# Linear attention with staged weights: bias copies issued later, the next head's weights loaded a piece per chunk, the scores' transpose placed further back

## The reference, cut to what matters

```python
u = h @ w_in                                  # q, k, v, r and a low-rank gate a1
glog = log_sigmoid(a1 @ w_a2 + b_a) / GLA_TAU
bc = cumsum(glog)                             # in a chunk
o_inter = (q * exp(bc)) @ S
att[t, s] = sum_d q[t, d] * k[s, d] * exp(bc[t, d] - bc[s, d])     # s <= t
o = o_inter + att @ v
S = exp(b_last) * S + (k * exp(b_last - bc)).T @ v
out = (rmsnorm(o) * norm_g * silu(r)) @ w_out
```

## Time and profile before

| | |
|---|---|
| median of three runs | 2278.31 us (2277.18 to 2278.43) |
| the profiled execution's own time | 2276.93 us |
| its span, first to last instruction | 2275.2 us |
| TensorE matmuls busy | 2171.4 us (95%), 12858 instructions |
| TensorE's mean granted clock | 0.983 of full speed |
| VectorE, ScalarE, GpSimd busy | 1386.6, 1137.7, 1046.7 us |
| linear attention in the span | from 756 to about 1433 us |

### The profile page before, as it was taken

One profiled execution on the slowest core, in us unless ns is written; L12 is line 12 of the kernel. 1 busy time (PEld: TensorE's weight loads), 2 busy tenths in 40 slices (PEclk: granted clock), 3 DMA queues, 4 the chain that ended last, 5 costly groups with the idle time before them and its releaser, 6 DMA issues. The chain is left out here.

```text
span 2275.2 us, 34224 instructions
## 1 busy us (share of the span) xinstructions
PE 2171.4 (95%) x12858; PEld 1089.0 (48%) x12858; DVE 1386.6 (61%) x2174; ACT 1137.7 (50%) x2165; POOL 1046.7 (46%) x790
## 2 busy tenths in 40 slices
PE   8999999999899869999999999899899997999998
PEld 4555555553444434454444444344455553444443
DVE  6999999987564424534544444567558884345322
ACT  7766666676773424433444534333358885334111
POOL 2988888887888121212112121276248886000000
PEclk9999999999999889999999999899999999999999
DMA  5011011033344320121301113365536664103222
GB/s 217 29 47 47 27 45 43 27 117 119 103 137 169 77 56 18 53 52 17 88 16 28 22 30 69 107 161 144 153 72 121 120 103 78 45 10 102 84 101 93
DMA packets 237723, 178.99 MB, mean 79 GB/s; under 512 B 188847, under 2 KB 208943, under 8 KB 236536
## 3 DMA queue, kind: packets, MB, share of 16 engines
q1 hardware_dynamic: 237560, 176.81, 28.9%
HBM read 96.65 MB, written 35.80 MB: 58 GB/s over the span
## 5 line engine op out<-in xcount | busy, mean ns | idle before, releaser
L1179 DVE SCALAR_TENSOR_TENSOR cv_tap_sum<-cv_glu,cv_prm,cv_tap_sum 128x1024 f32<-128x1024 f32 x326 | 418.9, 1288 | 11.9 <-ACT cv_tap_sum L667 2.4
L932 POOL TENSOR_TENSOR mixed<-mixed,cv_tap_products 128x1024 f32<-128x1024 f32 x153 | 364.0, 2379 | 77.7 <-ACT cv_tap_products L682 62.2
L101 PE MATMUL cv_proj<-H_hi,cv_w_ga 128*128 128x416 f16 (+1 forms) x640 | 217.0, 339 | 8.1 <-DVE H_lo L1152 8.1
L102 PE MATMUL cv_proj<-H_lo,cv_w_ga 128*128 128x416 f16 (+1 forms) x640 | 217.0, 339 | 0.0
L103 PE MATMUL cv_proj<-H_hi,cv_w_ga 128*128 128x416 f16 (+1 forms) x640 | 217.0, 339 | 0.0
L101 PE MATMUL gm_vr<-gm_wvr_hi,H_hi 128*128 128x512 f16 x512 | 194.7, 380 | 0.0
L102 PE MATMUL gm_vr<-gm_wvr_lo,H_hi 128*128 128x512 f16 x512 | 194.0, 379 | 0.0
L103 PE MATMUL gm_vr<-gm_wvr_hi,H_lo 128*128 128x512 f16 x512 | 194.0, 379 | 0.0
L1978 POOL TENSOR_TENSOR gm_q_inter<-gm_q_rel,gm_block_decays 128x512 f32<-128x512 f32 x16 | 16.8, 1047 | 350.1 <-ACT gm_block_decays L2068 350.1
L2084 ACT ACTIVATE gm_v_r<-gm_vr 128x256 f16<-128x256 f32 x68 | 26.0, 383 | 291.8 <-PE gm_vr L103 271.4
L682 ACT ACTIVATE cv_tap_products<-cv_glu,cv_prm 128x1024 f32<-128x1024 f32 x138 | 151.6, 1138 | 35.8 <-POOL mixed L932 35.7
(11 more groups left out here) (470 smaller groups left out, 5540.1 us busy)
## 6 DMA issues: line engine op xcount, KB each, us to landing
cv_w_stage<-conv_w SPq DMA_DIRECT2D x24, 512.0 KB, 4.0
mixed<-gla_w SPq DMA_DIRECT2D x8, 1024.0 KB, 8.4
go_rows<-h_rows SPq DMA_DIRECT2D x16, 512.0 KB, 4.2
h_rows<-go_rows SPq DMA_DIRECT2D x16, 512.0 KB, 3.2
pl_sums_a<-h_rows SPq DMA_DIRECT2D x16, 512.0 KB, 3.5
out<-pl_sums_a SPq DMA_DIRECT2D x16, 512.0 KB, 2.6
cv_tap_products<-gate_z SPq DMA_DIRECT2D x24, 256.0 KB, 4.6
mixed<-xT SPq DMA_DIRECT2D x12, 416.0 KB, 8.3
```

What stands on the lines that cost most here:

```text
L101: nc.tensor.matmul(out, w_hi, x_hi, start=first, stop=False)
L102: nc.tensor.matmul(out, w_hi, x_lo, start=False, stop=False)
L932: nc.gpsimd.tensor_tensor(c_unit(U), c_unit(U), prod[:, r % 3, :], ALU.add).then_inc(s_add, 1)
L1179: nc.vector.scalar_tensor_tensor(out=acc_unit(U), in0=window(U, k), scalar=col(U // 2, k), in1=acc_unit(U), op0=ALU.mult, op1=ALU.add).the ...
```

## The change

It has four parts. (a) The table's eight rows are written to the first part of w_stage instead of v_r's slot 4, and ScalarE's wait before chunk 4 falls away. The DMA that copies them to DRAM is issued in slot 2 of SyncE's order, behind the key transposes of the first two groups. (b) The next head's weights are loaded one MB at a time: head 1's where R is chunk 3, 4 and 5 of head 0, head 2's and 3's where R is chunk 14, 15 and 16 of the head two before; head 3's last four pieces go together where R is chunk 16, after a wait for the copies' end, since two of them go into w_stage. (c) In a slot with eight steps the transpose of the scores comes after five steps instead of four, in a slot with four steps after three instead of two. (d) At a change of head it comes after 16 of the 24 short matmuls instead of ahead of them.

```diff
-        oh, rb, vec = vr[0:33, 2, :], vr[0:33, 3, 0:HEADS], vr[0:HEADS, 4, :]
+        oh, rb, vec = vr[0:33, 2, :], vr[0:33, 3, 0:HEADS], wst[0:HEADS, 0, :]
...
-                sp.wait_ge(s_bs, 1)
-                rows = bass.AP(copies.tensor, copies.offset, [[(P + 1) * PITCH, HEADS], [PITCH, P + 1], [1, PITCH]])
-                sp.dma_start(rows, spread_rows(vec, P + 1)).then_inc(s_bo, 16)
-
-                def load_head(hd):
+
+                def spread_bias():
+                    sp.wait_ge(s_bs, 1)
+                    rows = bass.AP(copies.tensor, copies.offset, [[(P + 1) * PITCH, HEADS], [PITCH, P + 1], [1, PITCH]])
+                    sp.dma_start(rows, spread_rows(vec, P + 1)).then_inc(s_bo, 16)
+
+                def load_wide(hd, a):
                     sp.wait_ge(s_wl, 2 + PIECES * hd)
-                    for a in range(0, PIECES if hd < GH - 1 else WIDE_PIECES, 4):
-                        sp.dma_start(room(hd, a, a + 4), w_heads[hd, :, a * NPIECE:(a + 4) * NPIECE]).then_inc(s_ww[a // 4], 16)
-                    if hd == GH - 1:
-                        for q in range(WIDE_PIECES, PIECES):
-                            sp.dma_start(staged(hd, q), w_heads[hd, :, q * NPIECE:(q + 1) * NPIECE]).then_inc(s_wp[q - WIDE_PIECES], 16)
+                    sp.dma_start(room(hd, a, a + 4), w_heads[hd, :, a * NPIECE:(a + 4) * NPIECE]).then_inc(s_ww[a // 4], 16)
+
+                def load_last(hd):
+                    sp.wait_ge(s_bo, 16)
+                    for q in range(WIDE_PIECES, PIECES):
+                        sp.dma_start(staged(hd, q), w_heads[hd, :, q * NPIECE:(q + 1) * NPIECE]).then_inc(s_wp[q - WIDE_PIECES], 16)
...
-                load_head(1)
                 earlier = []
...
                     earlier = before
+                    if i == 2:
+                        spread_bias()
                     if R:
                         hd, c = R[0], R[2]
+                        if hd == 0 and c in (3, 4, 5):
+                            load_wide(1, 4 * (c - 3))
                         if c == 10 and hd + 1 < GH:
                             load_gate(hd + 1)
-                        if c == 13 and hd + 2 < GH:
-                            load_head(hd + 2)
+                        if c in (14, 15, 16) and hd + 2 < GH:
+                            if hd + 2 == GH - 1 and c == 16:
+                                load_last(GH - 1)
+                            else:
+                                load_wide(hd + 2, 4 * (c - 14))
...
-                    if cc == 4:
-                        act.wait_ge(s_bo, 16)
...
                     if c == 0:
-                        for work in between:
-                            work()
                         for a, b in ((0, 0), (1, 0), (0, 1)):
+                            for work in between if b else []:
+                                work()
                             for k in ks:
...
-                        for work in between if k == ks[len(ks) // 2] else []:
+                        for work in between if k == ks[-(3 * len(ks) // 8)] else []:
                             work()
```

## The result

| | before | after |
|---|---|---|
| median of the runs | 2277.86 us (4 runs, 2277.18 to 2278.43) | 2254.11 us (4 runs, 2252.40 to 2256.25) |
| ratio, 95% interval | | 0.9892 [0.9880, 0.9904] |
| profiled execution | 2276.93 us | 2253.43 us |
| its span | 2275.2 us | 2251.7 us |

The profiled executions differ by 23.5 us, and it is these that the following rows explain. Both enter the linear attention at the same time: its first matmul, which the view of waits calls `gm_logit`, stands at 757.50 before and 757.52 after, so times of the two traces can be set side by side. One run of the kernel before, among those made for the experiments, took 3263.74 us at a granted clock of 0.652 and is left out of every median.

What follows compares the result with a forecast made beforehand. TensorE, busy 95% of the span, was taken as the bound. 21.3 + 0 + 3.9 + 0.3 + 0 = 25.5 us off the profiled 2276.93 gives 2251.4, for the median 2252.8 us; range 2249 to 2258.

Steps and rivals of the forecast that it cites:

- (a): Copies behind the first key transposes: TensorE's 19.15 us wait and 2.2 us of lower clock after it go, 21.3 us.
- (b): Weights loaded a piece per chunk: nothing gained, since nothing waited, and nothing lost, 0.
- (c): Transpose a step later: six waits in eight-step slots give 3.9 us, half slots with the last chunk 0.3 us.
- (d): At the three changes of head, 16 short matmuls put into the 2.27 us wait give 0; bounds 0 and 0.3 each.
- Rival A: A new wait between 801 and 812 takes over half of the long one, 10 us back: 2263, chance 0.05.
- The copies' other end: Copies run from 786 to about 828 and hold row 1's transposes, with about 20 us of cover: costs nothing.
- both slower rivals: Behind the copies: rows lose their cover, 2319, chance 0.02; or a small hold of 3 to 6 us, 2256 to 2259, 0.08.
- The half slots: Six four-step slots: 0.3 us gained in a first half, 0.37 lost in a second; a pair is even.
- The waits for attT_lo: Sign in the profile after: a new TensorE wait, six or more times, with about 0.3 us each.

Runs made afterwards that it cites:

- e2: The changed kernel with the bias copies back at the front of the queue, ahead of the first key transposes: 2269.06 us, ratio 0.9959.
- e3: The changed kernel with head 1's three weight loads back at the front of the queue, the copies still in slot 2: 2253.61 us, ratio 0.9892.
- e10: The kernel before with the later transpose of part (c) alone: 2275.0 us in one run.
- e8: The kernel before with part (d) alone, the transpose moved among the short matmuls: 2277.53 us in one run.
- e11: The changed kernel with four more pairs of the small bias-table matmul at the stage's start: 2259.59 us in one run.
- e4: The changed kernel with parts (c) and (d) undone: 2259.60 us, ratio 0.9918.
- e12: The same program as e4, profiled once more: 2259.25 us in a single run.

## Why the prediction came out

The time was 2254.1 us where 2252.8 was forecast, within the range, and faster as forecast; for the profiled execution 23.5 us instead of 25.5. The largest term and its mechanism were right. That the total came so close is in part luck: 4.4 us lost to the clock at the changes of head, which the forecast had at nothing, met 2.6 us of small gains that it had not either (0.6, 0.3, 0.8 and 0.9 below). Point by point:

- **(a)** 21.3 us, as forecast: the wait's 19.15 whole, and 2.15 against 2.2 for the clock behind it. The trace shows 21.9, with the 0.6 of the stage's entry that are the execution's. e2 and e3 take the two suspected causes of the wait apart. Rival A, a new wait in the place of the old, did not come: GpSimd had k_state at 780.67.
- **The copies' other end.** They were issued at 785.33 (forecast 786), row 1's transposes at 821.49 (822) and held till 831.0 (828). They had landed by about 834, and ScalarE wrote row 4's high half at 847.90 without a wait, so some 14 us of the cover stood, and both slower rivals fell. The Trainium skill's rule on the order of a ring ("DMA: Bandwidth & Descriptors", the section on queues, rings and completion order) agrees with that hold, 5.30 and 4.14 us, and with e2's 17.35 and 9.51. It cost nothing because the victims had time.
- **(b)** 0 as forecast, shown for head 1 by e3, which gives the same time with the loads back at the front. For head 2 and 3 it rests on the list of waits, which has none for a DMA.
- **(c)** 3.9 us for six waits, exactly: 0.65 each, in after as in e10. Beside them 0.11 us each in the three slots behind these, 18.06 instead of 18.17, 0.3 in all, in e10 too, where (c) stands alone; the forecast had left them out. The half slots gave -0.2 instead of +0.3; the forecast's two effects, 0.3 gained in a first half and 0.37 lost in a second, were 0.26 to 0.37 and 0.40. The forecast's +0.3 took in the last chunk, whose transpose did come 0.40 earlier: with it the term is +0.2. The rest of the 1.3 on the way out of the stage, 0.9, the forecast did not have, as it followed nothing past the last transpose. The waits for attT_lo came ten times, with 3.1 us in all; the six in the half slots are 0.15 each, where about 0.3 was forecast.
- **(d)** This is the step that failed: that the change at a change of head "gives 0, three times". The edit itself gives 0.28 us each, 0.8 in all, as e8 and e11 show where the clock holds; the bound of 0.9 had it, the value taken did not. But the three changes of head took 3.6 us more than before, not 0. The forecast looked for a fall of the clock only behind the long wait, and none at the changes of head, where the profile before shows none. In the last chunk it does show one, as the 0.42 us of the row at 1432.62 tell, and that row was passed over. The waits there stayed, 1.54 us and a new one of 0.47 behind it instead of 2.27 alone, and the clock fell behind all three in this profile: -4.4 us, plus the 0.8.

The sum as it was: 21.3 + 0.6 + 3.9 + 0.3 + 0.8 - 4.4 - 0.2 + 1.3 - 0.1 = 23.5.

What stays open is why the kernel before fell at no change of head in two profiles and the changed kernel at all three. With the odds of the 36, six without a fall would be rare; e8 and e10, nearly the same program as before, fell once and twice. The runs show that no single part of the change is needed for a fall and that it differs between executions; they do not show what sets it, nor whether part (a) has a share in it (5 of 15 against 18 of 21).

## What to carry to other kernels

The transfer over eight partitions was slow itself, 48 to 50 GB/s, and held the transposes behind it on its queue: put such a transfer where the work behind it has cover, and count that cover. The waits at a change of head cost twice what their idle time alone does (1.58 us and some 1.5 more), because the clock may fall behind them; cost such a wait with and without the fall, and don't read its absence in one profile as safety. When a wait for another engine remains, look at what that engine does just before: here the order of two of VectorE's jobs was worth 10 us, nearly half of what the whole change gave.

## What the runs showed of the hardware that was not expected

- The granted clock went to 0.50 behind waits of 1.54 and 0.47 us that stand close together, for 3 us or so (after), and kept 1.00 behind the same waits at two changes of head of e11. Behind a single wait of 2.27 or 2.28 us it kept 1.00 in e4 and fell in e12, the same program.
- It also fell to 0.50, from 771.7 to 777.7 us, behind ten matmuls of 33*8 that had kept TensorE busy without a gap from 767.2 on (e11).
- The copies' 2064 KB from eight partitions took 44 to 46 us whether 3 MB of loads ran beside them (before) or not (e2 and after), at 48 to 50 GB/s and a share of 0.45 to 0.47 of the 16 DMA engines. The Trainium skill, in "DMA: Bandwidth & Descriptors", in the section on why a DMA increments its semaphore by 16, says that a DMA runs on the largest number of engines up to 16 that divides the slowest dimension of both sides, which for eight rows is eight; the share, just below one half, agrees.
- Behind the copies a DMA transpose took 4 to 17 us to issue instead of 1.22, and three loads 23.24 us instead of 1.40.
